# Neighbourhood attention row by row: quarter-array scores, one softmax pass, 64-column value products, three rows in flight

## The reference, cut to what matters

```
s_band = einsum('brqhd,brikhd->bhrqik', qg, kg) * scale
s_band = where(col_ok, s_band + bias, -inf)
s_ctx  = einsum('brqhd,blhd->bhrql', qg, k_ctx) * scale
p = softmax(concatenate([s_band.reshape(B, H, rows, GRID_W, kr * GRID_W), s_ctx], axis=-1))
o = einsum('bhrqik,brikhd->brqhd', p_band, vg) + einsum('bhrql,blhd->brqhd', p_ctx, v_ctx)
na = o * silu(gate)
```

## Time and profile before

| | us |
|---|---|
| median of three runs | 3594.04 |
| span of the profiled execution, first to last instruction | 3594.1 |
| attention stage, 2848 to 3171 | 323 |
| its row loop, first scores to last gate product | 2875.6 to 3155.5 |
| TensorE busy between 2900 and 3141 | 217 of 241 |

### The profile page before, as it was taken

How to read it: one execution, slowest core, us unless ns; L and a number is a source line. 1 busy time by engine, 2 the same in 40 slices (tenths; PEclk the granted TensorE clock), 3 DMA queues, 4 the chain that set the end, 5 groups by cost and what they waited for, 6 DMA issues and landing times. The chain is left out here.

```text
span 3594.1 us, 52496 instructions
## 1 busy us (share of the span) xinstructions
PE 3055.7 (85%) x19078; PEld 2499.5 (70%) x19078; DVE 1460.2 (41%) x2731; ACT 1071.3 (30%) x2149; POOL 239.3 (7%) x153
## 2 busy tenths in 40 slices
PE   6499999999999999968888888888845488959899
PEld 2388888888888888757777777777833266648677
DVE  1511111110000000067665666566556555557533
ACT  2311111112222222233434343434322255520122
POOL 1300000000000000020000000000000170020121
PEclk8699999999999999979988898889967699979899
DMA  6112222222222222100000000000033510067643
GB/s 205 53 57 76 68 72 71 71 70 70 71 71 71 71 71 71 61 24 25 27 20 16 18 27 20 17 18 16 10 97 110 182 60 0 0 221 269 234 135 128
DMA packets 172434, 267.21 MB, mean 74 GB/s; under 512 B 24426, under 2 KB 130538, under 8 KB 157546
## 3 DMA queue, kind: packets, MB, share of 16 engines
q1 hardware_dynamic: 169962, 256.52, 21.9%
q10 hardware_dynamic: 2304, 8.39, 0.6%
HBM read 162.64 MB, written 102.25 MB: 74 GB/s over the span
## 5 line engine op out<-in xcount | busy, mean ns | idle before, releaser
L383 PE MATMUL proj_ps<-h_hi,w_hi 128*128 128x512 f32 (+1 forms) x1976 | 772.3, 391 | 11.8 <-ACT w_hi L286 11.8
L383 PE MATMUL proj_ps<-h_lo,w_hi 128*128 128x512 f32 (+1 forms) x1976 | 770.1, 391 | 0.0
L337 DVE TENSOR_TENSOR w_lo<-w_raw,w_hi 128x128 fp32r<-128x128 f32 x472 | 128.9, 290 | 1135.0 <-ACT w_hi L286 1134.8
L383 PE MATMUL proj_ps<-h_hi,w_lo 128*128 128x512 f32 (+1 forms) x1976 | 589.2, 391 | 0.0
L383 PEld LDWEIGHTS proj_ps<-h_hi,w_hi 128*128 128x128 f32 x1976 | 372.2, 188 | 100.2 <-ACT w_hi L286 12.2
L383 PEld LDWEIGHTS proj_ps<-h_lo,w_hi 128*128 128x128 f32 x1976 | 372.2, 188 | 86.6
L383 PEld LDWEIGHTS proj_ps<-h_hi,w_lo 128*128 128x128 f32 x1976 | 367.4, 188 | 82.9
L286 ACT CAST w_hi<-w_raw 128x128 fp32r<-128x128 f32 x472 | 132.3, 299 | 798.1 <-PE proj_ps L383 594.3
L875 PE MATMUL rw_ps<-inv,m_b 128*128 128x128 f32 x1440 | 206.3, 304 | 37.9 <-DVE inv L721 37.9
L875 PEld LDWEIGHTS rw_ps<-inv,m_b 128*128 128x128 f32 x1440 | 195.9, 219 | 50.2 <-DVE inv L721 50.2
L832 ACT COPY inv<-rw_ps 128x512 f32<-128x512 f32 x144 | 84.3, 585 | 465.6 <-PE rw_ps L875 465.5
(11 more groups left out here) (285 smaller groups left out, 4466.1 us busy)
## 6 DMA issues: line engine op xcount, KB each, us to landing
scratch_gatesT<-z_stage SPq DMA_DIRECT2D x32, 1024.0 KB, 4.8
m_gate<-scratch_gatesT SPq DMA_DIRECT2D x32, 1024.0 KB, 5.2
w_raw<-in_w_in SPq DMA_DIRECT2D x59, 512.0 KB, 5.5
scratch_zT<-z_stage SPq DMA_DIRECT2D x16, 1024.5 KB, 4.8
scratch_zT<-z_stage SPq DMA_DIRECT2D x11, 1153.5 KB, 5.3
ada<-in_ada_w SPq DMA_DIRECT2D x6, 2048.0 KB, 18.7
x_rows<-in_x SPq DMA_DIRECT2D x8, 1024.0 KB, 5.0
mb_raw<-scratch_branchT SPq DMA_DIRECT2D x16, 512.0 KB, 5.5
```

Of the source, the lines that this page charges most:

```text
L337: nc.vector.tensor_tensor(w_lo[:, k, :], w_raw[:, k, :], w_hi[:, k, :].bitcast(F32), ALU.subtract).then_inc(w_lo_ready, 1)
L383: return nc.tensor.matmul(out, w[:, k, :], h[:, k, cols], start=first, stop=last)
```

## The change

- **Scores.** `q_t` is scaled in place, in two pieces (L1490). For each pair and head a product of 64 rows and 64 output partitions runs on one quarter of the array: pair 0 on the two diagonal quarters, pair 1 on the other two (`side`). There are four products of 512 columns and four of 256 per row, into PSUM banks 0 and 1 (pair 0) and 2 and 3 (pair 1). The partitions of `q_heads` that held zeros are gone.
- **Softmax.** A window of bias, 512 columns followed by 256 zeros, is laid out by GpSimd in `bias_windows`: one for the 25 interior rows, two slots for the seven edge rows. One custom instruction per pair then covers all 768 keys, and one exponential with one sum. The join and the addition of two sums are gone.
- **Values.** 24 products of 64 output partitions and 64 columns per row, alternating between the two halves of the output partitions, so that no unused blocks are computed. The scaled result is 128 x 128, turned back by one transpose; the gate buffer is laid out to suit and is loaded and stored in four pieces.
- **Order.** All 32 rows are written out, without a loop. In step n TensorE does the scores of row n, the values of row n-2, the turning of row n-1 and the turning back of row n-2; the turned probabilities have two buffers. SiLU of the gate moves from before row 0 to after row 1.
- **Pooling.** Its gate and weights take the memory of `v_t` and so are loaded after v has been turned; GpSimd begins the pooling after the window of row 3, and sets the windows of rows 29 to 31 after it.

TensorE in one row before: scores of pair 0 (L1566, L1567), turning back (L1602), turned probabilities of pair 0 (L1576), the same for pair 1, values (L1592).

The core of the diff:

```diff
+        side = lambda p, h: h if p == 0 else 1 - h
...
+        def window(r):
+            return 1 + EDGES.index(r) % 2 if r in EDGES else 0
...
 # GpSimd
-            nc.gpsimd.memset(qs[:], 0.0).then_inc(qz, 1)
+            nc.gpsimd.memset(wins[:, :, :, BAND:KEYS], 0.0).then_inc(wins_zero, 1)
...
+            def set_window(r):
+                win = place(r)[2]
+                nc.gpsimd.tensor_copy(wins[:, window(r), :, 0:BAND], bias[:, :, win:win + BAND]).then_inc(win_set, 1)
+            set_window(0)
+            set_window(1)
+            set_window(4)
+            for r in (2, 3):
+                fv.after(pool, r - 2, "b1")
+                set_window(r)
...
 # ScalarE
+            for cols in (slice(0, BLK), slice(BLK, SEQ)):
+                A.activation(q[:, :, cols], q[:, :, cols], ACT.Copy, scale=CH ** -0.5).then_inc(q_scaled, 1)
+            def exps(r, p):
+                fv.after(act, r, f"n{p}")
+                if p == 0 and r >= 2:
+                    bt.after(act, r - 2, "TC")
+                x = st[:, r % 4, p, :]
+                fs.done(A.activation(pr[:, r % 2, p, :], sall[:, p, :], ACT.Exp, bias=x[:, 1:2], accum_out=x[:, 2:3]), f"e{p}")
...
+            for n in STEPS:
+                if valid(n):
+                    exps(n, 0)
+                if valid(n - 1):
+                    copies(n - 1)
+                if valid(n):
+                    exps(n, 1)
+                if n == 1:
+                    act.wait_ge(loads["g"], 64)
+                    A.activation(ng[:], ng[:], ACT.Silu).then_inc(silu_done, 1)
...
 # VectorE
+            def front(r, p):
+                x = st[:, r % 4, p, :]
+                fp.after(dve, r, "S")
+                if r >= 1:
+                    fs.after(dve, r - 1, f"e{p}")
+                fv.own(dve, r, V.tensor_tensor_reduce(out=sall[:, p, :], in0=ps[:, 2 * p:2 * p + 2, :].rearrange("p b k -> p (b k)")[:, 0:KEYS],
+                                                      in1=wins[:, window(r), p, :], scale=1.0, scalar=-3e38, op0=ALU.add, op1=ALU.max,
+                                                      accum_out=x[:, 0:1]), f"b{p}")
+                fv.done(V.tensor_scalar(x[:, 1:2], x[:, 0:1], -1.0, None, ALU.mult), f"n{p}")
...
+                if valid(n - 2):
+                    r = n - 2
+                    fs.after(dve, r, "e1")
+                    bvr.own(dve, r, V.reciprocal(rsum[:], st[:, r % 4, :, 2]), "r")
+                    bo.after(dve, r, "O")
+                    by_pair = rsum[:, :].rearrange("p (m o) -> p m o", o=1).to_broadcast([P, 2, CH])
+                    bvr.done(V.tensor_tensor(on[:].rearrange("p (m c) -> p m c", m=2), ps[:, 7, 0:P].rearrange("p (m c) -> p m c", m=2),
+                                             by_pair, ALU.mult), "o")
+                if valid(n - 1):
+                    bt.after(dve, n - 1, "TC")
+                    bvc.done(V.tensor_copy(prt[:, (n - 1) % 2, :, BAND:KEYS], ps[:, 6, :].rearrange("p (m c) -> p m c", m=2)), "PC")
...
 # TensorE
+            def scores(r):
+                start = place(r)[0]
+                pe.wait_ge(q_scaled, 1 if (r + 1) * GRID <= BLK else 2)
+                if r >= 1:
+                    fv.after(pe, r - 1, "b1")
+                for c0, w, at in ((start * GRID + CTX, BAND, 0), (0, CTX, BAND)):
+                    for p in range(2):
+                        for h in range(2):
+                            o = ps[half(side(p, h)), 2 * p + at // BLK, 0:w]
+                            last = T.matmul(o, q[half(h), p, r * GRID:(r + 1) * GRID], k[half(h), p, c0:c0 + w], start=True, stop=True)
+                fp.done(last, "S")
...
+            def values(r):
+                start, odd, _ = place(r)
+                bs.after(pe, r, "P1")
+                bvc.after(pe, r, "PC")
+                if r >= 1:
+                    bvg.after(pe, r - 1, "g")
+                for p in range(2):
+                    for j in range(6):
+                        rows = ve[:, j - 4, :] if j >= 4 else vo[:, start // 2 + j, :] if odd else ve[:, 2 + start // 2 + j, :]
+                        for h in range(2):
+                            hd = side(p, h)
+                            last = T.matmul(ps[half(h), 7, p * CH:(p + 1) * CH], prt[:, r % 2, p, j * P + h * CH:j * P + (h + 1) * CH],
+                                            rows[:, p * P + hd * CH:p * P + (hd + 1) * CH], start=(j == 0), stop=(j == 5))
+                bo.done(last, "O")
...
+            for n in STEPS:
+                if valid(n):
+                    scores(n)
+                if valid(n - 2):
+                    values(n - 2)
+                if valid(n - 1):
+                    turn_probs(n - 1)
+                if valid(n - 2):
+                    bvr.after(pe, n - 2, "o")
+                    bot.done(T.transpose(ps[:, 7, BR:BR + P], on[:], s["ident"][:]), "OT")
```

More of the change, by code:

```diff
@@ L1367, in attention_stage @@
         half = lambda h: slice(h * CH, (h + 1) * CH)
+        side = lambda p, h: h if p == 0 else 1 - h
+        EDGES = [r for r in range(ROWS) if r < 4 or r > ROWS - 4]
         def place(r):
@@ L1372, in place @@
             return start, start % 2, (start - r + KR - 1) * GRID
[L1374 to L1387, removed]
+        def window(r):
+            return 1 + EDGES.index(r) % 2 if r in EDGES else 0
+        valid = lambda r: 0 <= r < ROWS
+        STEPS = range(ROWS + 3)
         @block.sync
@@ L1465, in _ @@
                 pool.sem_inc(diff_set, 1)
+            for r, before in ((ROWS - 3, 2), (ROWS - 2, 3), (ROWS - 1, ROWS - 3)):
+                fv.after(pool, before, "b1")
+                set_window(r)
         @block.scalar
@@ new lines, in copies @@
+            def copies(r):
+                for p in range(2):
+                    bt.after(act, r, f"T{p}")
+                    if p == 0 and r >= 2:
+                        bo.after(act, r - 2, "O")
+                    bs.done(A.copy(prt[:, r % 2, p, 0:BAND], ps[:, 4 + p, :]), f"P{p}")
+            for n in STEPS:
[8 more added lines that the diff above has]
+                    A.activation(ng[:], ng[:], ACT.Silu).then_inc(silu_done, 1)
@@ L1561, in _ @@
             pe.wait_ge(loads["k"], 32)
-            def scores(r, par, p, start):
-                fs.after(pe, r, "q1")
-                T.matmul(ps[:, p, :], qs[:, par, p, :], k[:, p, bass.ds(start * GRID + CTX, BAND)], start=True, stop=True)
-                fp.done(T.matmul(ps[:, 2 + p, 0:CTX], qs[:, par, p, :], k[:, p, 0:CTX], start=True, stop=True), f"S{p}")
-            def turn_probs(r, par, p):
-                fs.after(pe, r, f"c{p}")
-                if p:
-                    bv.after(pe, r, "P0")
-                for j in range(6):
-                    to = ps[:, 4 + p, j * P:(j + 1) * P] if j < 4 else ps[:, 6, p * CTX + (j - 4) * P:p * CTX + (j - 3) * P]
-                    last = T.transpose(to, pr[:, par, p, j * P:(j + 1) * P], s["ident"][:])
-                bp.done(last, f"T{p}")
@@ L1596, in step @@
-            def step(r, at, before, at_before, last, par):
-                if r is not None:
-                    scores(r, par, 0, at[0])
-                if last is not None:
-                    bv.after(pe, last, "o")
-                    for p in range(2):
-                        ins = T.transpose(ps[:, 7, BR + p * P:BR + (p + 1) * P], on[:, p, :], s["ident"][:])
-                    bp.done(ins, "OT")
-                if before is not None:
-                    turn_probs(before, 1 - par, 0)
-                if r is not None:
-                    scores(r, par, 1, at[0])
-                if before is not None:
-                    turn_probs(before, 1 - par, 1)
-                    for p in range(2):
-                        values(before, p, *at_before)
@@ new lines, in turn_probs @@
+            def turn_probs(r):
+                for p in range(2):
+                    fs.after(pe, r, f"e{p}")
+                    for j in range(4):
+                        last = T.transpose(ps[:, 4 + p, j * P:(j + 1) * P], pr[:, r % 2, p, j * P:(j + 1) * P], s["ident"][:])
+                    bt.done(last, f"T{p}")
+                for p in range(2):
+                    for j in range(2):
+                        last = T.transpose(ps[:, 6, p * CTX + j * P:p * CTX + (j + 1) * P], pr[:, r % 2, p, BAND + j * P:BAND + (j + 1) * P], s["ident"][:])
+                bt.done(last, "TC")
```

148 lines of the change are left out of this document (49 added, 99 removed).

## The result

The changed kernel takes 3482.42 us (median; 3479.64 to 3485.51), where the kernel before took 3594.89 in the same comparison: a ratio of 0.969 with a 95% interval of 0.968 to 0.970. The forecast was 3480. Its profiled execution spans 3482.1 us, 112.0 less than before.

A forecast was written before the change was run, and what follows sets the result against it. TensorE's passes in order plus a few hand-overs were taken to bound each row. Passes of 4.61 us plus 0.19 wait made 4.8 per row; with beginning and end the gain was 113.7, giving 3480 us, range 3465 to 3498 (8 in 10: 3462 to 3515).

The forecast's parts named there:

- The passes: TensorE's row: scores 1.46, values 1.56, twelve transposes 1.32, transpose back 0.27, sum 4.61 us.
- The four-fold overlap: Scores on TensorE: four quarters run side by side, 1.29 us plus 0.17 for the switch, instead of 5.16 without overlap.
- The wait for VectorE: Transpose back waits for VectorE's softmax and output scaling, 3.07 us after the scores against TensorE's 2.88: row 0.19 longer, 4.8.
- The beginning: First rows near half speed, then SiLU with two table loads, 6.2 us; scores of row 4 start at 2901, 3 us either way.
- The first scores start where they did: Start of row 0: first scores as before, at 2875.6 plus 0.4 us for a longer scaling.
- The end: From the scores of row 31 at 3030.5 to the last gate: 11.3 us, ending at 3041.8.
- Stays as it is: Behind the row loop: pooling products, stores and two stages take as long as before.
- Small terms: GpSimd beside the row loop: window copies 1.8 us each, pooling ending near 2965 instead of 2953.4, at no cost.
- The two-quarter rival: Scores: diagonal quarters sharing a PSUM bank cannot run together; scores 2.58, row 6.1, program 3517 us; chance 0.09.
- the strict order: TensorE passes start and end strictly in program order; row 7.4 us, program 3555 us; chance 0.03.
- The new wait between engines: Row hand-overs: two-pair softmax 0.5 to 1 us longer than summed; row 5.3 to 5.8, program 3495 to 3509 us; chance 0.06.
- the half clock: Row loop: TensorE's short bursts fall to the 1.2 GHz level; row 9.0 us, program 3602 us; chance 0.03.

The follow-up runs named there:

- e3: Changed kernel with every value product computing its 64 columns twice, into 128 columns, the second copy unused: 3514.61 us, row 5.79 us.
- e5: Changed kernel with an unused VectorE reciprocal of 128x32 elements added ahead of the reciprocal of the sums: 3486.59 us, row 4.88 us.
- e9: Changed kernel with gate loaded first, SiLU before row 0, and the gate in two transfers over all 128 partitions instead of four over 64: 3496.13 us.
- e1: Changed kernel with both pairs' scores on the same two diagonal quarters, so two quarters work at a time: 3517.81 us, row 5.93 us.
- e2: Changed kernel with the same sixteen score passes ordered quarter by quarter in the program: 3482.46 us, row 4.72 us.

## Why the prediction was right, and which terms were off

**The passes.** Predicted 1.46 + 1.56 + 1.32 + 0.27 = 4.61. Measured 1.45 + 1.55 + 1.37 + 0.20 = 4.57, where the last two terms are those of e3, whose transpose back doesn't wait. The two large terms are right to 0.01 us, each for the reason given: taking the overlap away in one of them costs nearly what was computed (1.26 us for 1.29, 1.22 for 1.2) and leaves the other alone. The four-fold overlap taken from the earlier trace rows held, also where two quarters write one bank, which no row of before had shown.

**The wait for VectorE.** Predicted 0.19 us, measured 0.10 (4.67 against 4.57); the step was right (the scaled output sets the transpose back, as e5 shows) and its size was not. One pair's start to start is 1.11 us (2961.07 to 2962.18), not 1.21: behind the custom instruction the small step takes 0.11 from start to start (2962.07 to 2962.18), where 0.2 had been taken from the earlier trace rows. Two pairs: 0.20 us; against that the first softmax starts 0.24 us after the scores (2960.83 to 2961.07), where 0.1 was taken. Row for row it is 4.67 us for 4.80, and 27 times 0.13 are 3.5 us to the good.

**The beginning.** Predicted 2901 for the scores of row 4, measured 2903.31: SiLU's hold was counted, the half clock after the idle time it causes was not (the values of row 1 start at 2897.73, for which 2897.5 was computed). "The first scores start where they did" was wrong too, and hidden by luck: from the stage's first load to the first scores it takes 30.70 us (2846.44 to 2877.14), before 27.30 (2848.28 to 2875.58), but the stage happened to begin 1.84 us earlier. What the loads cost there was not taken apart. The hole varies: the gap between rows 3 and 4 was 11.06 us here and 9.67 in another run of the same kernel.

**The end.** Predicted 11.3 us from the last scores to the last gate, measured 12.48 (3029.48 to 3041.96). The values of a row wait for the gate product of the row before, because both use one bank; in the loop the next scores cover that, in the last two rows nothing does:

```profile
3035.09 1.62 PE L1615 MATMUL na_ps<-v_even,probs_t 128*64 128x64 f32 x48 [0.86 <-DVE na_gate L1539]
...
3039.24 1.62 PE L1615 MATMUL na_ps<-v_even,probs_t 128*64 128x64 f32 x48 [0.96 <-DVE na_gate L1539]
```

That the last gate ends at 3041.96, where 3041.8 was predicted, is luck in this respect: 2.3 us late at the beginning, 3.5 early in the rows, 1.2 late at the end.

**Behind the loop.** "Stays as it is" was wrong by 2.1 us. The gate store is now four transfers over 64 partitions each. SP's queue, the changed kernel, and then before:

```profile
3041.99 5.50 SPq L1415 DMA_DIRECT2D scratch_branchT<-na_gate  x4
...
3059.82 0.38 SPq L1676 DMA_DIRECT2D mw_raw<-in_w_br  x1
```

```profile
3155.56 0.37 SPq L1415 DMA_DIRECT2D scratch_branchT<-na_gate  x1
...
3171.28 0.38 SPq L1660 DMA_DIRECT2D mw_raw<-in_w_br  x1
```

From the last gate to the next stage's first DMA: 15.8 us before, 17.9 after. The windows of the stores (DMA share and GB/s last), the changed kernel and before:

```profile
3042.00:3052.00 10.00, 7.26 (x16) 2.87 (x16) 5.64 (x8) 1.33 (x1) 0.00 (x0) 1.00 0.92 197
```

```profile
3156.00:3165.00 9.00, 6.93 (x16) 2.57 (x14) 5.64 (x8) 0.73 (x1) 0.00 (x0) 1.00 0.56 233
```

The same bytes keep the DMA engines at 0.92 instead of 0.56, at fewer GB/s. The loads ahead of the loop show it more plainly. The changed kernel while its four gate transfers land, and the kernel before while its loads over 128 partitions do, the gate's among them:

```profile
2872.00:2878.00 6.00, 0.86 (x4) 0.34 (x8) 0.00 (x0) 2.06 (x2) 0.77 (x1) 0.53 1.01 198
```

```profile
2870.00:2876.00 6.00, 0.42 (x1) 0.45 (x2) 0.00 (x0) 0.61 (x2) 4.30 (x31) 0.58 1.02 423
```

With the engines as busy, less than half the bytes move. The bias, which the rival of e9 blamed, had landed by 2862.91, when GpSimd began to mask it. "2 MB as before" counted bytes, not the form of the transfers. That it is the 64 partitions, and not the number of transfers, is likely but not shown: no run changes one alone. The rest of the account: 111.7 us from the stage's first load to the last gate, and 2.4 us less in the stages before and behind, which the change does not touch; 111.7 - 2.1 + 2.4 are the 112.0 of the span. So the 3480 for 3482 is right by the row loop, and to the last two microseconds by chance.

**Small terms.** A window copy by GpSimd took 1.04 us, not 1.8; pooling ended at 2964.0 (2965 predicted); nothing of it came into the path.

**The rivals.** The two-quarter rival was built (e1) and the strict order refuted (e2), each by a kernel of its own. The Trainium skill's two rules behind them (TensorEngine Tiling (Array Packing), Gotcha 1; TensorE: Matmul & The Clock Gate, The mechanism) do not hold as worded for this case: four quarters started within 20 ns while two of them, of different row halves, wrote different partitions of bank 0, and passes did start ahead of earlier ones of another quarter (e2). The new wait between engines did not come beyond the 0.10 us above, and the half clock did not come: the granted clock was 1.00 from 2903 on.

## What to carry to other kernels

Price a packed loop by passes on the array: the longest chain in one quarter, plus a switch wherever the tile form changes (here 0.16 us behind the scores, 1.45 for 1.29, and behind the values, 1.55 for 1.39), and then compare it with the chain through the slowest other engine: here the two were a tenth of a microsecond apart. Look beside the loop: an instruction ahead of it that leaves TensorE idle (here SiLU on ScalarE) cost twice, by the wait of 3.96 us and by some 2 us at the lower clock after it. When a tile's layout changes, look at each DMA that reads or writes it, and not at its bytes alone: here four transfers over 64 partitions moved 198 GB/s where others moved 423, and an outermost dimension of two left one transfer at 49.

## What the runs showed of the hardware

In the trace of before, a VectorE instruction on two columns, which else takes 0.16 us, three times took 2.5 to 2.8 us. The first:

```profile
2897.58 2.71 DVE L1533 TENSOR_TENSOR softmax_rsum<-softmax_stats 128x2 f32<-128x2 f32 x1
```

and GpSimd at that time:

```profile
2895.75 4.52 POOL L1463 TENSOR_TENSOR pool_diff<-pool,pool_in 64x2048 f32<-64x2048 f32 x1
```

The VectorE instruction ended at 2900.29, when GpSimd's subtraction of two tiles ended (2900.27). The other two (2921.03 and 2929.66) ended likewise within 0.02 us of a GpSimd instruction with two operands. All of them read two operands from SBUF. The Trainium skill (GPSIMD Engine Reference, 1. Specifications) names contention of GpSimd with VectorE instructions that have two such inputs; these rows agree, with some 2.5 us lost to VectorE at a time. The changed kernel adds the sums of band and context nowhere, so it has no such instruction in the loop, and the longest VectorE step of this size there lasted 0.16 us. It gained little by that: in the kernel before, the rows that started from 2899 to 2932 lasted 7.87, 7.88, 8.00, 8.52 and 8.38 us, those without a stall 7.80 to 7.88 written out and 8.27 to 8.41 in the loop, so two rows were longer, by about 0.1 us each.
